# A two-layer diffusion trunk step: row-tiled attention scores, negated queries, adaLN chunks moved to another stage, and one block of differential scores per head

## The reference, cut to what matters

```
mod = silu(c) @ w_ada[l] + b_ada[l]        # 6 x 1024: shift1, scale1, gate1, shift2, scale2, gate2
h = rmsnorm(x, norm_mix) * (1 + scale1) + shift1
u = h @ w_in                               # hyena 3x512 | NA q,k,v | DA q,k,v | gates 3x1024
y_hy = hyena(u_hy)                         # short conv, two long convolutions by DFT
# neighbourhood attention, 8 heads of 64, latent tokens:
s = q k^T / 8 + bias, masked to a column window; s_ctx = q k_ctx^T / 8; softmax over both; @ v
# differential attention, 8 heads, two maps of width 32 each:
a = softmax(q1 k1^T / sqrt(32)) - lam * softmax(q2 k2^T / sqrt(32));  o = rmsnorm(a @ v) * (1 - lam_init)
merged = sum_b sigmoid(u_gate_b) * (y_b @ w_lift_b);  x += gate1 * (merged @ w_out)
x += gate2 * swiglu_ffn(rmsnorm(x, norm_ffn) * (1 + scale2) + shift2)
```

## Time and profile before

| | |
|---|---|
| runs | 3244.84 us median of 3 (3239.64 to 3246.84) |
| profiled execution | 3243.62 us, of which the traced span is 3241.8 us |
| TensorE busy | 2960.7 us (91%), mean granted clock 0.946 |
| VectorE / ScalarE / GpSimd busy | 1506.6 (46%) / 584.4 (18%) / 1563.9 us (48%) |
| chain that ended last | TensorE 77%, VectorE 14%, ScalarE 3% |

### The profile page before, as it was taken

The page is one execution under the profiler, slowest core; times in us unless marked ns, Lnnn a source line. Parts: engine busy times, 40 slices in busy tenths (PEclk is TensorE's granted clock), DMA queues, the critical chain, the costliest instruction groups (busy, mean ns, idle before and its releaser), DMA issues.

```text
span 3241.8 us, 42762 instructions
## 1 busy us (share of the span) xinstructions
PE 2960.7 (91%) x17564; PEld 2614.0 (81%) x17564; DVE 1506.6 (46%) x2553; ACT 584.4 (18%) x1189; POOL 1563.9 (48%) x588
## 2 busy tenths in 40 slices
PE   5898689998979998999998989998979998999997
PEld 1447659895569997999997959896569997999997
DVE  6885871645742214448653572655741124420113
ACT  1123110314520002000102111313520002100100
POOL 1003407061027765778775707061027765777764
PEclk8899799998979998999998999998989998999998
DMA  4434323020002222335432223020002222322222
GB/s 176 136 120 160 91 80 98 4 75 17 1 28 77 75 70 92 110 112 174 147 108 87 72 78 95 11 69 23 1 27 72 79 67 96 99 72 72 79 69 75
DMA packets 76790, 258.86 MB, mean 80 GB/s; under 512 B 9107, under 2 KB 12691, under 8 KB 75060
## 3 DMA queue, kind: packets, MB, share of 16 engines
q1 hardware_dynamic: 49148, 176.96, 17.3%
q10 hardware_dynamic: 27448, 79.17, 7.1%
HBM read 237.75 MB, written 18.35 MB: 79 GB/s over the span
## 4 chain that ended last, share of the span: by engine, by line
PE 77%; DVE 14%; ACT 3%; issue 2%; DMA 2%; DVEq 1%; ACTq 1%; POOLq 0%; POOL 0%
PE PS L446 57%; PE PS L467 3%; PE PS L726 3%; DVE adap L1179 3%; PE PS L530 2%; PE PS L748 2%; PE PS L674 1%; PE PS L735 1%; PE PS L645 1%; PE PS L500 1%; PE PS L613 1%; DVE mx L1473 1%; PE PS L658 1%; PE PS L720 1%; DVE yt L1334 1%
## 5 line engine op out<-in xcount | busy, mean ns | idle before, releaser
L428 POOL TENSOR_SCALAR whi<-wraw 128x1024 fp32r<-128x1024 f32 x292 | 838.2, 2870 | 1606.3 <-PE PS L446 1538.6
L446 PE MATMUL PS<-hhi,whi 128*128 128x320 f32 x3072 | 717.9, 315 | 66.6 <-DVE hlo L1163 43.3
L430 POOL TENSOR_TENSOR wlo<-wraw,whi 128x1024 fp32r<-128x1024 f32 x292 | 725.6, 2485 | 43.0
L446 PE MATMUL PS<-hlo,whi 128*128 128x320 f32 x3072 | 710.5, 313 | 0.0
L446 PE MATMUL PS<-hhi,wlo 128*128 128x320 f32 x3072 | 710.2, 313 | 0.0
L446 PEld LDWEIGHTS PS<-hhi,whi 128*128 128x128 f32 x3072 | 522.2, 192 | 80.9 <-issue 32.5
L446 PEld LDWEIGHTS PS<-hlo,whi 128*128 128x128 f32 x3072 | 523.9, 192 | 0.0
L446 PEld LDWEIGHTS PS<-hhi,wlo 128*128 128x128 f32 x3072 | 523.1, 191 | 0.0
L1179 DVE CUSTOM_DVE_ANT_0 adap<-ada,cond 128x1024 f32<-128x1024 f32 x192 | 338.7, 1764 | 35.0 <-DMA ada<-in_w_ada 12.8
L1562 DVE SCALAR_TENSOR_TENSOR x<-PS,mod,x 128x128 f32<-128x128 f32 x144 | 54.5, 433 | 300.0 <-PE PS L446 300.0
L1595 DVE TENSOR_TENSOR gact<-silu,PS 128x640 f32<-128x640 f32 x44 | 36.1, 821 | 334.8 <-ACT silu L1129 334.8
(11 more groups left out here) (233 smaller groups left out, 4044.8 us busy)
## 6 DMA issues: line engine op xcount, KB each, us to landing
wraw<-in_w_strips SPq DMA_DIRECT2D x292, 512.0 KB, 3.6
ada<-in_w_ada ACTq DMA_DIRECT2D x72, 512.0 KB, 4.5
ada<-in_w_ada SPq DMA_DIRECT2D x24, 512.0 KB, 3.9
spectra<-hst ACTq DMA_DIRECT2D x48, 256.0 KB, 2.0
hld<-spectra ACTq DMA_DIRECT2D x8, 768.0 KB, 5.1
hld<-spectra ACTq DMA_DIRECT2D x12, 512.0 KB, 3.6
cond<-conds ACTq DMA_DIRECT2D x3, 1024.0 KB, 4.8
x<-in_x_in SPq DMA_DIRECT2D x1, 2560.0 KB, 14.7
```

Source lines behind the costliest of these rows:

```text
L428: nc.gpsimd.tensor_scalar(hi, raw, 1.0, None, ALU.mult)
L430: nc.gpsimd.tensor_tensor(lo, raw, hi, ALU.subtract).then_inc(w_split, 1)
L446: ins = pe.matmul(out[:, h, :], w[:, kt, :], mv[:, h * HALF:(h + 1) * HALF], start=start and m == 0, stop=stop and m == 2)
```

## The change

- The 16 adaLN chunks of layer 0 leave the convolution strips. `cond[1]` and three (was four) chunk buffers are now loaded after the convolution's last output and the neighbourhood caches; ScalarE issues two more loads after each evacuation of a neighbourhood strip, and VectorE makes all 16 chunks between the bias expansion and the first `na_max`.
- In layer 0, for strips `S_NA + 1` to `S_NA + 11`, ScalarE instead of GpSimd makes the high half (`strip_hi`); GpSimd waits for it and makes the low half.
- Neighbourhood scores are made for two heads at a time, each from its own 64 rows of `naq` and `nak`, four PSUM banks in turn. Queries carry the factor -0.125, mask and bias are negated, the maximum becomes a minimum, and the exponential has scale -1, so that the minimum is its bias without a negation. `nqz`, `nmx` and their instructions go.
- Differential scores likewise: queries carry -`DA_SCALE`, each map uses its own 32 rows. The latent keys of the second map are split so that both maps lie at one distance (`DA_MAP` = 896), for one reduction and one difference of 640 columns. Cached keys are laid out zero-extended (`dckb`, 1 MB a layer instead of 256 KB) against the full 128 rows of queries. All five products of head n+2 stand between turn and value product of head n.

```diff
-ADA_SLOTS = (2, 4, 4)
+ADA_SLOTS = (2, 3, 4)
+HI_ON_ACT = range(S_NA + 1, S_NA + N_NA)
...
 # gpsimd
+                if n in HI_ON_ACT:
+                    pool.wait_ge(w_hi, n - HI_ON_ACT.start + 1)
+                else:
+                    pool.wait_ge(w_in[n % 3], 16 * (n // 3 + 1))
...
 # tensor, neighbourhood
+                def na_scores(u):
...
+                        for out, r in heads:
+                            pe.matmul(out[:, lat], identb[:, :], maskb[:, MASK0[j]:MASK0[j] + nb, :],
+                                      start=True, stop=False)
+                        for out, r in heads:
+                            pe.matmul(out[:, lat], naq[r, ch, qb * 128:qb * 128 + 128],
+                                      nak[r, ch, C + b0 * 128:C + (b0 + nb) * 128], start=False, stop=True)
+                    for out, r in heads:
+                        pe.matmul(out[:, cache] if qb else out[:, 0:128], naq[r, ch, qb * 128:qb * 128 + 128],
+                                  nckT[r, ch, :] if qb else nak[r, ch, 0:C], start=True, stop=True).then_inc(s_ns, 1)
...
-                    if n + 1 < 40:
-                        na_scores(n + 1)
+                    if n % 2 == 0 and n + 2 < 40:
+                        na_scores(n // 2 + 1)
                     na_turn(n)
...
 # tensor, differential: da_scores(n)
+                    r1, r2 = (slice(64 * (h % 2) + 32 * m, 64 * (h % 2) + 32 * m + 32) for m in range(2))
+                    q1, q2 = (daq[r, ch, qb * 128:qb * 128 + 128] for r in (r1, r2))
...
+                    pe.matmul(PS[:, b, :], q1, dak[r1, ch, C:T], start=True, stop=True)
+                    pe.matmul(PS[:, b + 2, 0:384], q2, dak[r2, ch, C + 128:T], start=True, stop=True)
+                    pe.matmul(PS[:, b + 1, 384:512], q2, dak[r2, ch, C:C + 128], start=True, stop=True)
...
 # da_cache_scores(n)
+                    pe.matmul(PS[:, b + 1, 0:128], q, k[:, 0:128], start=True, stop=True)
+                    pe.matmul(PS[:, b + 2, 384:512], q, k[:, 128:256], start=True, stop=True).then_inc(s_ds, 1)
...
                 for n in range(40):
-                    if n + 2 < 40:
-                        da_scores(n + 2, True)
                     da_turn(n)
                     if n + 2 < 40:
-                        da_scores(n + 2, False)
+                        da_scores(n + 2)
+                        da_cache_scores(n + 2)
                     da_pv(n)
...
 # scalar, after the caches of the neighbourhood attention are issued
+                if lay == 0:
+                    act.dma_start(cond[1][:, :, :], conds).then_inc(s_cond[0], 16)
+                    for k in range(ADA_SLOTS[1]):
+                        ada_load(1, k, (lay, N_ADA1 + k))
+                def strip_hi(n):
+                    if n in HI_ON_ACT:
+                        act.wait_ge(w_in[n % 3], 16 * (n // 3 + 1))
+                        act.wait_ge(w_used, n)
+                        A(whi[n % 2][:, :, :], wraw[n % 3][:, :, :], ACT.Copy).then_inc(w_hi, 1)
                 for n in range(8):
+                    strip_hi(lay * STRIPS + S_NA + n + 1)
                     act.wait_ge(s_nq, nth(lay, s_nq, n + 1))
-                    dst, sc = (naq, 0.125) if n < 4 else (nak, 1.0)
+                    dst, sc = (naq, -0.125) if n < 4 else (nak, 1.0)
                     A(halves(dst[:, n % 4, :]), pair((n + 3) % 4), ACT.Copy, scale=sc).then_inc(s_nqe, 1)
+                    for k in range(2 * n + 3, min(2 * n + 5, N_ADA2 - N_ADA1)):
+                        if lay == 0:
+                            ada_load(1, k, (lay, N_ADA1 + k))
...
 # vector
+                if lay == 0:
+                    dve.wait_ge(s_cond[0], 16)
+                    for k in range(N_ADA2 - N_ADA1):
+                        ada_dot(1, k, N_ADA1 + k)
+                    modulation(lay, N_ADA1, N_ADA2)
+                    norm_scale(lay, 1)
                 for n in range(40):
                     na_max(n)
...
                 def da_max(n):
+                    p0, q = 3 * 512 * (n % 2) + (0 if n // HEADS else 512), 2 * (n % 2)
+                    keys = 640 if n // HEADS else 128
+                    dve.wait_ge(s_ds, nth(lay, s_ds, n + 1))
+                    both = PSF[:, p0:p0 + 2 * DA_MAP].rearrange("p (m n) -> p m n", m=2)
+                    V.tensor_reduce(mx[:, q:q + 2], both[:, :, 0:keys], AX, ALU.min).then_inc(s_dm, 1)
```

More of the change, by code:

```diff
@@ L205, in build @@
         dcv = at("dcv", 123.5, [128, BW])
-        dckT = at("dckT", 125.5, [128, KB, 128])
-        dqz = [at(f"dqz{i}", 127.5 + 2 * i, [128, 4, 128]) for i in range(2)]
+        dckb = at("dckb", 125.5, [128, KB, 512])
         dp1 = [at(f"dp1{i}", 133.5 + 5 * i, [128, 640]) for i in range(2)]
@@ L628, in _ @@
                 pe.wait_ge(s_nve, nth(lay, s_nve, 5))
[L630 to L649, removed]
@@ new lines, in na_scores @@
+                def na_scores(u):
+                    qb, ch = u // 4, u % 4
+                    heads = [(PS[:, (2 * u + i) % 4, :], slice(64 * i, 64 * i + 64)) for i in range(2)]
+                    if u >= 2:
+                        pe.wait_ge(s_np, nth(lay, s_np, 2 * u - 2))
+                    if qb:
+                        j = qb - 1
+                        b0, nb = NA_BLOCKS[j][0], len(NA_BLOCKS[j])
+                        lat0, cache0 = (128, 0) if j == 3 else (0, nb * 128)
+                        lat, cache = slice(lat0, lat0 + nb * 128), slice(cache0, cache0 + 128)
+                        for out, r in heads:
[7 more added lines that the diff above has]
+                                  nckT[r, ch, :] if qb else nak[r, ch, 0:C], start=True, stop=True).then_inc(s_ns, 1)
@@ L963, in _ @@
                 for n in range(12):
-                    if n and lay == 0:
-                        for k in range(2 * n + 2, min(2 * n + 4, N_ADA2 - N_ADA1)):
-                            ada_load(1, k, (lay, N_ADA1 + k))
                     act.wait_ge(s_u, nth(lay, s_u, n + 1))
@@ L1509, in _ @@
                         da_max(n + 2)
-                    if n % 2 == 1 and (n + 5) // 2 < 20:
-                        da_queries((n + 5) // 2)
                 da_out(39)
@@ L1718, in constants @@
             ok = (ck[None, :] >= c0[:, None]) & (ck[None, :] < c0[:, None] + BLK)
-            mask[:, MASK0[j] + r, :] = np.where(ok, 0.0, NEG)
+            mask[:, MASK0[j] + r, :] = np.where(ok, 0.0, -NEG)
     n["maskb"] = mask
@@ L1787 @@
         n[k] = g[k][0].reshape(DEPTH, 128, KB, 128).transpose(0, 3, 2, 1)
+    apart = np.zeros((DEPTH, 4, 32, KB, 4, 128), np.float32)
+    for m in range(4):
+        apart[:, m, :, :, m] = n["cache_da_k"][:, 32 * m:32 * m + 32]
+    n["cache_da_k"] = apart.reshape(DEPTH, 128, KB, 512)
     flat = g["na_rpb"].reshape(DEPTH, HEADS, 15 * 31)
```

158 lines of the change are left out of this document (59 added, 99 removed).

## The result

The changed kernel takes 3380.41 us (median of 4 runs, 3375.47 to 3382.09) against 3243.12 us: ratio 1.042, 95% interval 1.040 to 1.044. Slower, as forecast, but by 137 us and not by 33; it lies 50 us above the top of the range. The profiled execution took 3379.79 us, its span is 3378.0.

A forecast was written before the change was run, and what follows sets the result against it. Bounds: ScalarE's blocked in-order queue (layer 0 convolution strips), TensorE (neighbourhood attention), a three-engine ring (differential attention). Sum -41.5 + 20 - 17 + 61 + 10 = +32.5 on 3243.6: 3277 us, slower; range 3228 to 3330.

The forecast's parts named there:

- the clock: TensorE's granted clock in the differential heads: some six falls to the lower level, 2.3 us more a head, +10 us.
- the ring: Differential attention's loop over three engines, turn to turn: 4.54 us a head before, 5.50 forecast.
- its rival: Clock falls all through the differential heads, half of them at the low level: about +74 instead of +10, 3341 us; chance 0.09.
- Part 4: Differential scores: all scores of head n+2 enter the ring, +0.96 us for each of 64 long heads, +61 us.
- The allowance for the change between tiled and whole products: Differential scores: 0.1 us a head in the ring; without it the term would be +55 us.
- Full concurrency as a rival: Row tiles run fully at once: ring +27, neighbourhood scores -26, in all -20 us, 3225 us; chance 0.16.
- break-even of 5.14 us: Differential heads: the ring must stay under this for the change to be faster, 4.54 + 38.5 / 64.
- Part 1: Layer 0 convolution: adaLN chunks leave its strips, first transpose 38.5 us earlier, transforms 3.0 us shorter, together -41.5 us.
- The 3.0 us in the transforms: Layer 0 convolution after its strips: 84.8 us falls to layer 1's 81.8, as it starts without idle time and low clock.
- Part 2: Layer 0 neighbourhood strips: ScalarE's new duties delay strips 13 (9.7 us) and 14 (5.4), plus cold starts and rest, +20 us.
- Part 3: Neighbourhood scores for two heads at a time: -8.5 us a layer, -17 in all.
- Three-pass overlap: Neighbourhood scores: two heads' four passes take the time of three, 0.96 us for 1.28.

The follow-up runs named there:

- full_rows: Changed kernel with the latent score products of the differential (DA) heads on all 128 rows instead of 32 (scores not the reference's): 3349.93 us.
- latents_before_turn: Changed kernel with the 32-row latent scores of DA head n+2 issued before the turn of head n, the cache scores behind it: 3305.33 us.
- dense_filler: Changed kernel with seven dummy products on all rows ahead of the 32-row latent scores of each long DA head: 3358.07 us.
- old_da: Changed kernel with the whole DA unit of the kernel before: 3197.70 us, ratio 0.985.
- rows64_first: latents_before_turn with the two latent maps on rows 0 to 63 and 64 to 127 (scores not the reference's): 3166.19 us.
- full_rows_first: latents_before_turn with the latent products on all 128 rows (scores not the reference's): 3186.47 us.

## Why the prediction went wrong

**The failed step is the clock.** "I add 10 us, some six falls" was worth, in the trace, the DA heads' +182.9 us less what the ring costs at the upper level. That ring is 5.30 us, so (5.30 - 4.54) x 64 = 49, and the other 134 us are the clock, an estimate. The price of a head at the lower level was nearly right, 7.40 - 5.30 = 2.1 us for the 2.3 forecast; wrong was the number of heads, all 64 and not the four or so that 10 us pay for. The reason why I had given its rival 0.09 was that "the low clock stretches TensorE's work so that it has hardly any idle time and recovers". On full rows the clock does recover, head by head, in full_rows. With both latent products on 32 rows the argument is false: TensorE had no idle time at all in latents_before_turn and stayed at 1.2 GHz. The premise behind it, that busy time as the profile counts it decides the clock, came from rows that hold no tiled product; nothing in the trace of the kernel before could have shown it. The rival itself, 3341 us with half the heads at the low level, named the right quantity and was nearest to the result.

**Part 4** had the order and the ring right and the overlap wrong. It gave all scores of a head 1.28 + 0.43 + 0.1 = 1.81 us; at the upper level they take 790.59 to 792.21 (the first value product) = 1.62, the maps side by side. The pair of maps alone takes 1.07, half way between the forecast's 1.28 and the 0.85 of full overlap: both products start together, but each pass of 512 columns lasts 0.54 us (790.59 to 791.13) for 0.43 on full rows. +49 instead of +61. The allowance for the change between tiled and whole products fits: the cache products stand 0.32 us apart in dense_filler (791.66 to 791.98) and 0.22 in full rows (797.63 to 797.85), so 0.10; it may be the drain that the Trainium skill names (TensorEngine Tiling (Array Packing), Key Properties), which gives no figure.

**Full concurrency as a rival** was right that the maps run side by side, but not in its price: its break-even of 5.14 us was not reached even at the upper level. There the change would have been +49 against the -45 that old_da shows for the rest, a draw and not a gain, and the clock came on top.

**Part 1** was right: first transpose 359.01 (360.7 forecast), transforms 84.3 us against 84.8, -40.7 in all against -41.5. The 3.0 us in the transforms did not come, although the clock did (0.93 to 0.98), so the low clock was not the reason for them; the strips gave more instead.

**Part 2** was right in each wait and its reason (9.5 and 5.2 us for 9.7 and 5.4), and 7 us too high in the sum, since the NA strips grew by 13.0 us (57.6 to 70.6) and not by 20: 4 us for cold starts and 1 for the rest were too much.

**Part 3**: from the first turn to the last the NA attention takes 69.2 and 69.5 us instead of 76.6 and 76.5, -14.4 against -17. Three-pass overlap was too careful: two heads' latent scores take 572.04 to 572.78 = 0.74 us, where three passes are 0.96 and full overlap 0.64. What hid it is the clock at the start of the attention, at its lower level for 17 and 20 us. The same NA code takes 65.7 and 66.9 us in old_da, where that stretch is 10 and 13 us long, and 65.7 to 72.6 over all kernels that have it; so the part is worth -20.5 in old_da. What sets the length of that stretch these runs don't tell, and each has one profiled execution. Its tiles have 64 rows, and behind that stretch they run at 1.00, which agrees with rows64_first.

Sum: -40.7 + 13.0 - 14.4 + 182.9 = +140.8 for 136.2 between the two spans; the 4.6 us left over are not assigned. What is measured is that the rows of the latent products decide the clock along with idle time. Whether it is the rows at work together, the height of a tile or the share of time with few rows, and where between 32 + 32 and 64 + 64 rows it turns over, was not settled. Nor was tried a DA unit with its reference result on 64-row tiles.

## What to carry to other kernels

Before putting products on fewer rows, read the granted clock of a trial, not the busy share: 32-row tiles that ran side by side lost to padded products here because they, and all work beside them, ran at half the clock. Zero padding is not waste if it keeps the clock. When an in-order queue is blocked, moving what stands behind the block mostly changes which instruction is late; here it took 15.3 us of idle time down to 6.8 at best. Making the awaited thing earlier was not tried.

## What was not expected of the hardware

TensorE 100% busy for 100 us with a granted clock of 0.50 (latents_before_turn), and 1.00 at 93% busy when only the rows of two products in each head changed (full_rows_first). The Trainium skill (TensorE: Matmul & The Clock Gate, Part 1: The HAM clock gate) ties the level to how busy TensorE has been lately; the runs agree for idle time and full rows (0.85 at 73% busy in full_rows), and show that with two 32-row products in each head the profile's busy share no longer tells the level. Dummy work on all rows made a kernel faster: 3358.07 against 3380.41 us.
